# The rows of seven expert pairs taken by matrix products from SBUF in place of gathers from DRAM, in a two-layer MoE encoder

## The reference

```
for l in range(DEPTH):
    x = x + attention_part(rms_norm(x, attn_norm_g[l]))
    x = x + hier_moe(rms_norm(x, ffn_norm_g[l]), routers, w_g[l], w_u[l], w_d[l])
return rms_norm(x, final_norm_g)

# hier_moe, for every expert e (combine is 0 where the token didn't choose e)
a = t @ w_g[e];  u = t @ w_u[e]
y += (silu(a) * u * combine[:, e]) @ w_d[e]
```

## Time and profile before

| | us |
|---|---|
| median of 3 runs | 1321.16 (1318.97 to 1321.61) |
| the profiled execution | 1318.96 |
| its span, first to last instruction | 1317.2 |
| TensorE (PE) busy | 1194.9 (91%) |
| VectorE (DVE) busy | 555.8 (42%) |
| ScalarE (ACT) busy | 408.7 (31%) |
| GpSimd (POOL) busy | 239.0 (18%) |
| mean granted clock of TensorE | 0.978 |

### The profile page before, as it was taken

The page is one execution under the profiler, slowest core; times in us unless marked ns, Lnnn a source line. Parts: engine busy times, 40 slices in busy tenths (PEclk is TensorE's granted clock), DMA queues, the critical chain, the costliest instruction groups (busy, mean ns, idle before and its releaser), DMA issues.

```text
span 1317.2 us, 17522 instructions
## 1 busy us (share of the span) xinstructions
PE 1194.9 (91%) x6408; PEld 793.1 (60%) x6408; DVE 555.8 (42%) x1392; ACT 408.7 (31%) x822; POOL 239.0 (18%) x177
## 2 busy tenths in 40 slices
PE   7999998999989999789599999899999999988981
PEld 5777777888877343233177777778887854433320
DVE  4557665433335322222355678553232453222115
ACT  5344456323242111001244444563332411110002
POOL 0324510222200111111012343102221011111100
PEclk9999999999999999899899999999999999999996
DMA  5433311653656999999833333126438489999995
GB/s 198 117 96 105 97 57 34 208 188 99 231 200 231 401 422 423 424 422 412 327 98 104 96 97 97 33 82 222 160 97 302 153 315 408 424 422 425 420 411 222
DMA packets 69152, 305.50 MB, mean 232 GB/s; under 512 B 11799, under 2 KB 12055, under 8 KB 58833
## 3 DMA queue, kind: packets, MB, share of 16 engines
q1 hardware_dynamic: 58624, 282.45, 56.9%
q0 software_dynamic: 10304, 21.23, 4.3%
q10 hardware_dynamic: 144, 0.77, 0.2%
HBM read 288.63 MB, written 23.07 MB: 237 GB/s over the span
## 4 chain that ended last, share of the span: by engine, by line
PE 69%; DMA 16%; SPq 5%; DVE 4%; ACT 3%; issue 2%; DVEq 1%; POOLq 0%; ACTq 0%
PE bank L540 14%; PE bank L542 14%; PE bank L541 13%; DMA gu<-in_gu_w 12%; PE bank L850 10%; PE bank L866 4%; SPq L401 4%; DMA raw<-in_stream 2%; PE bank L649 2%; PE bank L678 2%; SPq L406 2%; PE bank L613 1%; PE bank L782 1%; PE bank L820 1%; PE bank L845 1%
## 5 line engine op out<-in xcount | busy, mean ns | idle before, releaser
L850 PE MATMUL bank<-gu,xgt 128*64 128x512 f32 x1024 | 237.8, 614 | 39.6 <-DMA gu<-in_gu_w 38.4
L540 PE MATMUL bank<-h_hi,w_hi 128*128 128x512 f32 x640 | 253.0, 395 | 4.1 <-DVE h_lo L1290 3.4
L542 PE MATMUL bank<-h_hi,w_lo 128*128 128x512 f32 x640 | 249.4, 390 | 0.0
L541 PE MATMUL bank<-h_lo,w_hi 128*128 128x512 f32 x640 | 249.1, 389 | 0.0
L1245 DVE TENSOR_TENSOR w_lo<-raw,w_hi 128x1024 fp32r<-128x1024 f32 x102 | 133.6, 1311 | 174.3 <-ACT w_hi L978 174.2
L850 PEld LDWEIGHTS bank<-gu,xgt 128*64 128x64 f32 x1024 | 74.5, 141 | 197.1 <-issue 148.2
L540 PEld LDWEIGHTS bank<-h_hi,w_hi 128*128 128x128 f32 x640 | 120.2, 188 | 29.0 <-issue 5.3
L542 PEld LDWEIGHTS bank<-h_hi,w_lo 128*128 128x128 f32 x640 | 120.1, 188 | 25.3
L541 PEld LDWEIGHTS bank<-h_lo,w_hi 128*128 128x128 f32 x640 | 120.3, 188 | 23.8
L978 ACT ACTIVATE w_hi<-raw 128x1024 fp32r<-128x1024 f32 x102 | 107.4, 1053 | 59.7 <-PE bank L542 56.2
L866 PE MATMUL bank<-dn,zt 128*64 128x512 f32 x512 | 116.9, 598 | 6.0 <-ACT zt L1206 2.8
(11 more groups left out here) (189 smaller groups left out, 1601.0 us busy)
## 6 DMA issues: line engine op xcount, KB each, us to landing
gu<-in_gu_w SPq DMA_DIRECT2D x18, 4096.0 KB, 31.1
raw<-in_stream SPq DMA_DIRECT2D x112, 512.0 KB, 3.6
dn<-in_dn_w SPq DMA_DIRECT2D x18, 2048.0 KB, 31.7
gu<-in_gu_w SPq DMA_DIRECT2D x32, 1024.0 KB, 13.8
dn<-in_dn_w SPq DMA_DIRECT2D x20, 1024.0 KB, 19.0
gu<-in_gu_w SPq DMA_DIRECT2D x32, 512.0 KB, 5.1
swp<-pj SPq DMA_DIRECT2D x136, 64.0 KB, 2.2
dn<-in_dn_w SPq DMA_DIRECT2D x16, 512.0 KB, 5.8
```

Source lines behind the costliest of these rows:

```text
L540: mm(dst, ah, bh, start=start, stop=False)
L541: mm(dst, ah, bl, start=False, stop=False)
L542: return mm(dst, al, bh, start=False, stop=stop)
L850: last = mm(bank[b][e * CAP:(e + 1) * CAP, :], xgt[:, x_s, k, e * CAP:(e + 1) * CAP], gu[w_s][:, e, k, :], start=k == 0, stop=k == KD - 1)
```

## The change

For pairs 9 to 15 (BY_PE) of each layer the rows come as pair 0's do. GpSimd issues no gather for them. VectorE writes `placed` for pair n+2 in iteration n (n from 7 to 13), eight instructions for four tiles and two experts, after slots and before y_half(n). TensorE's rows_in waits for pl_ok in place of xg_ld and runs 32 products (4 tiles by 8 blocks) in place of 8 transposes. slot is made as before, since the scatters need it. The counts of the semaphores follow: 10 increments of pl_ok per layer, and xg_ld counted over the gathers that are left.

```
+BY_PE = range(9, PAIRS)
+PLACES = 3 + len(BY_PE)
 
                 def first_rows(t, l=l):
 
-                    pe.wait_ge(pl_ok, l * 3 + max(1, t))
+                    pe.wait_ge(pl_ok, l * PLACES + max(1, t))
+                    return placed_rows(t)
+
+                def placed_rows(t):
+
                     for k in range(KD):
                         last = mm(bank[2 + k // 4][:, (k % 4) * P:(k % 4 + 1) * P], x[:, t, k * P:(k + 1) * P], placed[:, t, :],
                                   start=t == 0 and k % 4 == 0, stop=t == TT - 1 and k % 4 == 3)
...
                 def rows_in(n):
-                    pe.wait_ge(xg_ld[n % 2], (l * (PAIRS // 2 - 1) + n // 2) * 16 if n % 2 == 0 else (l * (PAIRS // 2) + n // 2 + 1) * 16)
+                    if n in BY_PE:
+                        pe.wait_ge(pl_ok, l * PLACES + 3 + n - BY_PE.start + 1)
+                        pe.wait_ge(xtd_ok, 2 * (n0 + n))
+                        for t in range(TT):
+                            last = placed_rows(t)
+                        last.then_inc(xgt_ok, 1)
+                        return
+                    gathered = [m for m in range(1, PAIRS) if m not in BY_PE and m % 2 == n % 2]
+                    pe.wait_ge(xg_ld[n % 2], (l * len(gathered) + gathered.index(n) + 1) * 16)
                     pe.wait_ge(xtd_ok, 2 * (n0 + n))
                     turn(n % 2, xgt_ok)
...
-                def place(tiles):
+                def place(tiles, n=0):
 
                     for t in tiles:
                         for e in range(2):
-                            last = ts(placed[:, t, e * CAP:(e + 1) * CAP], c(C_IOTA, CAP), rankm[:, t, e:e + 1], rs[:, t:t + 1],
+                            last = ts(placed[:, t, e * CAP:(e + 1) * CAP], c(C_IOTA + n, CAP),
+                                      rankm[:, t, 2 * n + e:2 * n + e + 1], rs[:, t:t + 1],
                                       ALU.is_equal, ALU.mult)
                     last.then_inc(pl_ok, 1)
...
                     elif n + 3 < PAIRS:
                         dve.wait_ge(inf_ok, n0 + n + 4)
                         slots(n + 3, ix_ok)
+                    if n + 2 in BY_PE:
+                        place(range(TT), n + 2)
                     y_half(n)
...
                     pool.wait_ge(ix_ok, n0 + (n + 1 if n > 1 else 1))
-                    gather(n, xg_ld[n % 2])
+                    if n not in BY_PE:
+                        gather(n, xg_ld[n % 2])
```

## The result

The changed kernel takes 1356.55 us (median of 4 runs, 1354.69 to 1357.95), the kernel before 1320.88 beside it: a ratio of 1.027 (95% interval 1.0255 to 1.0285), 35.7 us slower. The forecast was 1354. The profiled execution took 1354.69 us with a span of 1352.9. Of all executions behind this text one, of the spread kernel of experiment 10, ran in a slower state (1432.44 us at a mean granted clock of 0.841), and its ratio leaves it out.

A forecast was written before the change was run, and what follows sets the result against it. The prediction took the DMA's loads of gu to bound the later expert stage before, TensorE after the change. Layers' +18.0 and +16.2 us, less 1.4, gave 32.8, so 1351.8; with 2.2 for the median, 1354 us, range 1347 to 1364.

The forecast's parts named there:

- which engine is the bound, and its pace: Expert stage from pair 8's up on: TensorE becomes the bound at 18.55 us a pair, against 15.9 for the DMA.
- the seven pairs' slack: Last seven pairs per layer: TensorE's waits for DMA, 24 to 26 us, some 3.5 a pair, can be spent for nothing.
- place costs nothing: VectorE after slots: writing placed adds 1.97 us per pair, covered by the down-projection with about 1 us left.
- the clock gives nothing back: TensorE in the expert stage: without waits it stays at full clock, but that gains no time.
- the earlier start of pair 8: Pair 8's up, no longer behind gather 9, starts 0.65 us earlier in the first layer, 0.55 in the second.
- the last scatter: End of the first layer: the last scatter takes 2.83 us, as in the second layer, instead of 4.26; -1.4 us.
- the price of a gather: DMA in the expert stage: each gather costs 0.65 us, so at most 9.1 us gained for 14 gathers.
- the rival in which the kernel gets faster: Expert stage: the DMA stays the bound, products fit in 4.5 us per pair; 1312 us, chance 3%.
- the first: Rival for the expert stage: the DMA stays the bound and the kernel is faster, 1312 us; chance 3%.
- second: Rival for TensorE's products: in one run of 64 they take about 5.2 us per pair; 1327 us, chance 3%.
- the third: Rival for TensorE's products: the clock falls in them, adding 14 x 1.7 = 24 us; 1378 us, chance 6%.

The follow-up runs named there:

- experiment 10: Changed kernel with products only for pairs 9, 11 and 13 of each layer, the other later pairs by gathers; 1318.18 us, ratio 0.9972 to the kernel before.
- experiment 3: Changed kernel with the seven gathers per layer issued and waited for as well, their rows unused; 1360.38 us, ratio 1.0288 to the kernel before.
- 6: Changed kernel with products of only two of the four token tiles for pairs 9 to 15; 1312.43 us, ratio 0.9944 to the kernel before.
- 7: Changed kernel with products of only three of the four token tiles for pairs 9 to 15; 1333.72 us, ratio 1.0096 to the kernel before.
- 4: Changed kernel with products only for pairs 9, 10 and 11, pairs 12 to 15 by gathers; 1317.17 us, ratio 0.9967 to the kernel before.
- 5: Changed kernel with products only for pairs 13, 14 and 15, the earlier ones by gathers; 1338.96 us, ratio 1.0143 to the kernel before.
- 9: Changed kernel with products only for pairs 9 to 12, four per layer; 1319.3 us, ratio 0.9988 to the kernel before.
- experiment 8: Changed kernel with VectorE writing placed twice for each pair, a drain between; 1357.24 us, ratio 1.0276 to the kernel before.
- experiment 1: Changed kernel with neither gathers nor products for pairs 9 to 15; 1307.83 us, ratio 0.9896 to the kernel before; run again, 1307.41 us.
- 2: Changed kernel without products, gathers of pairs 9 to 15 issued but leaving out every row but row 0; 1309.84 us, ratio 0.9913 to the kernel before.

## Why the prediction was right, point by point

The sum by stretches, from the two profiled executions. The end of pair 15's up is 638.88 and 1287.06 before, 657.39 and 1323.32 after.

| stretch | before | after | difference | forecast |
|---|---|---|---|---|
| start to pair 7's up, first layer | 506.95 | 506.60 | -0.35 | 0 |
| pair 7's to pair 8's up | 13.74 | 13.82 | +0.08 | -0.65 |
| pair 8's up to the end of 15's | 118.19 | 136.97 | +18.78 | +18.7 |
| to pair 7's up, second layer | 514.94 | 514.93 | 0.0 | -1.4 |
| pair 7's to pair 8's up | 13.09 | 14.03 | +0.94 | -0.55 |
| pair 8's up to the end of 15's | 120.15 | 136.97 | +16.82 | +16.7 |
| to the end of the span | 30.14 | 29.58 | -0.56 | 0 |
| sum | | | +35.7 | +32.8 |

**Right: which engine is the bound, and its pace.** The products took 7.25 us where I had 7.18, a pair 18.56 where I had 18.55, so the two main terms are within 0.1 us. That it is TensorE's queue alone shows in experiment 3 (gathers added back: the same 18.56 us a pair) and in 6 and 7 (16.77 us a pair for three tiles).

**Right: the seven pairs' slack is spent first.** 14 pairs of 6.2 us more would be 87 us; 35.7 came, since the DMA waits went. The runs of experiments 4, 5 and 9 show that budget: three pairs' products fit in it, four just fill it, and three at the end of the stage can't use it.

**Right: place costs nothing, the clock gives nothing back.** Shown by experiment 8 for the one. For the other, the window at full clock has the pace that was worked out from rows at full clock. Experiment 3 adds that a fall of the clock at pair 8 would still have cost 1.7 us, the size that the range allowed for.

**Mis-sized: the earlier start of pair 8.** I had taken 0.65 and 0.55 us off for gather 9. It did not come: pair 8 started 13.82 and 14.03 us after pair 7. Over all the kernels here that step took 13.09 to 14.80 us where gather 9 is issued (mean 13.9 over three kernels, two layers each) and 12.4 to 15.0 where it is not (mean 13.5 over ten executions). The means differ by 0.4 us the way that was forecast, but the scatter of a single execution is several times the term: the kernel of experiment 1 took 14.65 us in the second layer once and 12.38 the other time. These two terms, 2.2 us in sum, are the largest part of the miss. The 2.9 us between 35.7 and 32.8 are these 2.2, the 1.4 of the last scatter and 0.2 of the products, less 0.9 at the start and the end of the span for which no term was forecast.

**Mis-sized: the last scatter.** It did get shorter, but only half of the 1.4 us forecast reached the end of the layer, and none the experts of the next. From the timeline of all engines of the changed kernel, end of the first layer:

```profile
664.46 0.97 POOL L1772 DMA_INDIRECT y_rows<-yb,slot  x1 [11.40 <-DVE yb L1584]
...
665.19 4.87 DVE L1691 SCALAR_TENSOR_TENSOR x<-yld,small,x 128x1024 f32<-128x1024 f32 x4 [1.56 <-issue]
...
667.60 1.75 SPq L502 DMA_DIRECT2D yld<-y_rows  x4
...
669.98 2.35 DVE L1259 TENSOR_TENSOR w_lo<-raw,w_hi 128x1024 fp32r<-128x1024 f32 x2
672.43 4.87 DVE L1702 SCALAR_TENSOR_TENSOR x<-yld,small,x 128x1024 f32<-128x1024 f32 x4
```

The loads of y are issued 3.1 us after the scatter (664.46 to 667.60), where it was 4.3. But VectorE adds the first set of rows, splits two weight tiles (L1259) until 672.33 and starts the last addition at 672.43, without a gap: its own queue decides. That is 9.5 us after the copy of y (662.94), where before it was 9.1. The last addition then runs in one piece, where before its second half waited for y:

```profile
656.92 2.56 DVE L1685 SCALAR_TENSOR_TENSOR x<-yld,small,x 128x1024 f32<-128x1024 f32 x2 [0.81 <-DMA yld<-y_rows]
```

Counted from the copy of y, what follows the last addition starts after 14.3 us (677.22) and not 15.0 (659.41 there): 0.7 of the 1.4 us. From the copy to pair 0's up of the second layer it is 421.2 us in both kernels, so the 0.7 is lost again on the way; where, was not traced. The gain of one link was cut short by a second engine whose queue ended at nearly the same time.

**Mis-sized, without effect on the forecast: the price of a gather,** 0.90 us and not 0.65 (experiments 1 and 2). It enters only where the DMA is the bound, so the rival in which the kernel gets faster should have had some 1309 and not 1312.

The rivals: the first and second fall by the 7.25 us of the trace, the third (a fallen clock in the products) by the granted clock of 1.00 in the window above and by the same 18.56 us a pair in the second layer. The 81 ns per matmul that the Trainium skill gives (TensorE: Matmul & The Clock Gate, Back-to-back issue gap) is not what these fp32 products show: 113 ns per instruction and two instructions each.

## What to carry to other kernels

Where two engines race in a stage, compute each one's time per step and price a trade between them by the slower one: here 6.2 us of TensorE were paid per pair for 0.9 us of DMA, and it paid only as long as TensorE had waits to fill. Such slack is a sum over the steps that are left, not a right of each step: spend it early in the stage, where the engine can catch up on data that lands meanwhile, and stop before the engine's sum passes the DMA's. Take a gain on one link of the end for nothing until the next engine's queue there has been looked at.

## What the runs showed that was not expected

- A gather of about 64 rows of 4 KB, among weight loads at 420 GB/s, cost 0.90 us of the stream. A gather with nearly all of its 128 places empty cost about 0.1 or less, so the rows go at some 320 GB/s.
- The page's HBM line counts a row that is left out as read: with empty gathers it shows 288.63 MB as in the kernel before, 7.34 MB (14 x 128 rows of 4 KB) above the kernels without them, while the queue's own bytes fall.
- The time from pair 7's to pair 8's up, where TensorE first waits for weights, varied by 2.6 us over the executions without gather 9 (12.4 to 15.0 us), and by 2.3 us between two of the same kernel, while TensorE's own pace repeated to 0.01 us.
- After a wait of 2.25 us for weights an up took 8.78 us at a granted clock of 0.81 (7.09 at 1.00 in the changed kernel), in a stage in which TensorE was the bound from there on, and the whole of it showed in the start of the next pair.
